# Memory values made whole in the first expert stage, and cross attention that turns X itself

## The reference, cut to what matters

```
def cross_attention(hn, mem_n, w_cq, w_ckv, w_co):
    q = (hn @ w_cq).reshape(B, S, 4, 256)
    k, v = split((mem_n @ w_ckv).reshape(B, 256, 2, 4, 256))
    s = einsum(q, k) * 256 ** -0.5          # per head, 512 x 256
    p = softmax(s)
    return einsum(p, v).reshape(B, S, 1024) @ w_co

h = h + (g_a * (y_a @ w_proj_a) + g_b * (y_b @ w_proj_b)) @ w_out
h = h + cross_attention(rmsnorm(h, norm_cross), rmsnorm(mem, norm_mem), w_cq, w_ckv, w_co)
```

## Time and profile before

| | |
|---|---|
| median of 3 runs | 2379.2 us (2378.73 to 2381.66) |
| span of the profiled execution | 2375.1 us |
| instructions | 27530 |
| PE busy | 2154.3 us (91%) |
| DVE busy | 699.1 us (29%) |
| ACT busy | 361.6 us (15%) |
| POOL busy | 128.6 us (5%) |
| DMA | 533.20 MB, mean 224 GB/s |
| mean granted TensorE clock | 0.970 |

### The profile page before, as it was taken

One profiled execution on the slowest core, in us unless ns is written; L12 is line 12 of the kernel. 1 busy time (PEld: TensorE's weight loads), 2 busy tenths in 40 slices (PEclk: granted clock), 3 DMA queues, 4 the chain that ended last, 5 costly groups with the idle time before them and its releaser, 6 DMA issues.

```text
span 2375.1 us, 27530 instructions
## 1 busy us (share of the span) xinstructions
PE 2154.3 (91%) x11887; PEld 1077.8 (45%) x11887; DVE 699.1 (29%) x1761; ACT 361.6 (15%) x692; POOL 128.6 (5%) x158
## 2 busy tenths in 40 slices
...
GB/s 295 71 36 71 68 4 159 160 204 373 422 427 427 427 426 428 381 269 67 2 29 3 73 2 36 87 121 120 106 142 80 211 418 426 426 428 426 427 428 274
DMA packets 94159, 533.20 MB, mean 224 GB/s; under 512 B 11169, under 2 KB 26198, under 8 KB 66635
## 3 DMA queue, kind: packets, MB, share of 16 engines
...
## 4 chain that ended last, share of the span: by engine, by line
PE 64%; DMA 28%; DVE 5%; issue 1%; ACT 1%; ACTq 0%; SPq 0%; DVEq 0%; POOLq 0%
PE ps L198 61%; DMA RING<-in_w 7%; DMA SC<-in_w 6%; DMA RING<-in_w_e_gate 4%; DMA RING<-in_w_e_up 4%; DMA SC<-in_w_e_down 3%; DMA XT<-in_w_e_down 1%; DMA XT<-in_w 1%; DMA RING<-in_w_ckv 1%; DMA RING<-in_w_proj_a 1%; PE ps L367 0%; PE ps L2924 0%; PE ps L2337 0%; DMA SC<-xrows,ST 0%; DMA RING<-ytab 0%
## 5 line engine op out<-in xcount | busy, mean ns | idle before, releaser
L198 PE MATMUL ps<-SC 64*64 64x64 f32 (+5 forms) x5912 | 698.0, 325 | 70.9 <-DMA RING<-in_w_e_up 15.3
L198 PE MATMUL ps<-RING,SC 128*64 128x512 f32 (+2 forms) x1856 | 656.4, 610 | 75.3 <-DMA RING<-in_w_e_gate 23.3
L198 PE MATMUL ps<-XT,RING 128*128 128x512 f32 (+1 forms) x1104 | 488.7, 595 | 2.8 <-DVE XT L194 1.1
L198 PEld LDWEIGHTS ps<-SC 64*64 64x64 f32 (+3 forms) x5912 | 339.2, 143 | 320.0 <-issue 297.3
L198 PEld LDWEIGHTS ps<-RING,SC 128*64 128x64 f32 (+2 forms) x1856 | 232.6, 155 | 367.6 <-issue 363.2
L198 PEld LDWEIGHTS ps<-XT,RING 128*128 128x128 f32 (+1 forms) x1104 | 204.6, 189 | 246.2 <-issue 241.4
L1709 DVE TENSOR_TENSOR SC<-SC,ps 128x512 f32<-128x512 f32 x32 | 22.0, 687 | 689.2 <-PE ps L198 689.2
L198 PE MATMUL ps<-XT,SC 128*64 128x512 f32 (+1 forms) x344 | 158.0, 612 | 9.3 <-DMA SC<-in_w_e_up 4.9
L198 PE MATMUL ps<-RING,XT 128*128 128x512 f32 (+1 forms) x384 | 147.5, 541 | 0.0
L198 PEld LDWEIGHTS ps<-RING,XT 128*128 128x128 f32 x384 | 67.5, 190 | 74.3 <-issue 73.8
L198 PE MATMUL ps<-SC,RING 128*128 128x512 f32 (+1 forms) x320 | 90.3, 451 | 6.1 <-DMA RING<-in_w_proj_a 6.1
...
## 6 DMA issues: line engine op xcount, KB each, us to landing
RING<-in_w SPq DMA_DIRECT2D x41, 2048.0 KB, 33.2
SC<-in_w SPq DMA_DIRECT2D x41, 2048.0 KB, 33.2
RING<-in_w_e_gate SPq DMA_DIRECT2D x22, 2048.0 KB, 33.9
SC<-in_w_e_down SPq DMA_DIRECT2D x17, 2048.0 KB, 33.2
RING<-in_w_in SPq DMA_DIRECT2D x16, 2048.0 KB, 8.6
SC<-in_w_e_up SPq DMA_DIRECT2D x15, 2048.0 KB, 33.2
XT<-in_w SPq DMA_DIRECT2D x10, 2048.0 KB, 34.3
SC<-in_w_e_gate SPq DMA_DIRECT2D x10, 2048.0 KB, 33.6
```

The source lines that it names most:

```text
L198: return e.matmul(out, l, r, start=st, stop=sp, skip_group_check=True)
```

## The change

**1. V's left half moves to stage 0.** `mv_s` is called a second time, before pair 8's loads, for "cv0", and `mv_p`, `mv_a` make four more blocks after pair 7. `memV` is twice as wide; `memT` is gone with its four writes, its read, the load of "cv0" between the output products' and the cross attention's weights, and the products in `cr_p`.

**2. X itself is turned.** PE transposes X, not the normed X, tile by tile beside the output products (`g2*15 cr g2*2 cr g2*2 cr*5` in the plan). Per tile DVE copies the left half in one instruction with the gains, ACT the right half in four of 128x128, and ACT then squares the tile. The row's factor is made beside the q products and goes into the softmax: times 1/16 as the exponent's scale, and negative into the maximum.

**3. Places.** The ring's turns before the cross attention drop their last four, and stage 1's turn is (0, 1, 8, 4, 7, 5, 2, 3, 6).

```
-        W.wait_ge(*ME.on("ev", "xt", 6))
-        W.wait_ge(*ME.on("ev", "xt", 7))
-        for n in range(4):
-            e.dma_start(memT[:, n, :], me_homes[n]).then_inc(*ME.up("dmt", "memT"))
...
-                if put_n == 6 * 4 and bi == 0:
-                    mv_s(e)
+                if put_n in (6 * 4, 6 * 8) and bi == 0:
+                    mv_s(e, put_n // 24 - 1)
...
-                if bi == 0 and q == 3:
-                    for n in range(4):
+                if bi == 0 and q in (3, 7):
+                    for n in range(q - 3, q + 1):
                         mv_p(e, c, n)
...
-        slots.begin((0, 1, 0, 1, 0, 1, 2, 3, 0, 1, 2, 3, 0, 1, 2, 3))
+        slots.begin((0, 1, 0, 1, 0, 1, 2, 3, 0, 1, 2, 3))
...
-        wload(e, "cv0", t["w_ckv_2"][0], 1024, 512, (CR, ("w", "cv0")))
...
 def cr_p(e):
-        W.wait_ge(*CR.on("mem"))
-        for half in range(1):
-            W.wait_ge(*slots.on(f"cv{half}"))
-            for j in range(2):
-                b, free = c.take("v", half, j)
...
-        turn_p(e, cr)
-        xt_ready(e, c)
+        for tt in range(NT):
+            for hf in range(2):
+                b, free = c.take("xt", tt, hf)
                 W.wait_ge(*free)
+                W.wait_ge(*G2.on("X", tt))
+                for j in range(4):
+                    i = e.transpose(b[:, j * 128:(j + 1) * 128], X[:, tt, (4 * hf + j) * 128:(4 * hf + j + 1) * 128], ident[:, :])
+                i.then_inc(*c.up("p", "xt", tt, hf))
+            if tt < NT - 1:
+                yield
...
 def cr_a(e):
-        e.dma_start(SC[:, 1, :], memT.rearrange("p a n -> p (a n)")).then_inc(*c.up("dmem"))
-        for n in range(4):
+        for n in range(8):
             W.wait_ge(*ME.on("memV", n))
-        e.dma_start(cr_V[:, :, 512:1024], memV).then_inc(*c.up("dmem"))
+        e.dma_start(cr_V, memV).then_inc(*c.up("dmem"))
...
+        W.wait_ge(*G2.on("mix", 7))
+        for tt in range(NT):
+            W.wait_ge(*c.on("xt", tt, 1))
+            for j in range(4):
+                copy_a(e, XT[:, 4 + j, tt * 128:(tt + 1) * 128], c.at("xt", tt, 1)[:, j * 128:(j + 1) * 128], cr_gain[:, 4 + j:5 + j]).then_inc(*c.up("a", "ev", "xt", tt, 1))
+            W.wait_ge(*G2.on("X", tt))
+            W.wait_ge(*c.last("a"))
+            e.activation(SC[:, 10, 0:D], X[:, tt, :], AF.Square, accum_out=cr_ss[:, tt:tt + 1]).then_inc(*c.up("a", "sq", tt))
+            if tt < NT - 1:
+                yield
...
-                e.activation(cr_pb[u % 8], c.at("s", u)[:, 0:256], AF.Exp, bias=s[:, 0:1], scale=0.0625, accum_out=s[:, 1:2]).then_inc(*c.up("a", "ev", "s", u))
+                e.activation(cr_pb[u % 8], c.at("s", u)[:, 0:256], AF.Exp, bias=s[:, 0:1], scale=cr_rs[:, qt:qt + 1], accum_out=s[:, 1:2]).then_inc(*c.up("a", "ev", "s", u))
...
 def cr_v(e):
-        norm_v(e, cr)
...
+        mean_rsq_v(e, c, cr_R, "nrm", cr_ss, 1.0 / D, 1e-6)
+        W.wait_ge(*c.on("nrm", "rs"))
+        e.tensor_scalar(cr_rs, cr_R.y, 0.0625, None, A.mult).then_inc(*c.up("v"))
+        e.tensor_scalar(cr_nrs, cr_R.y, -0.0625, None, A.mult).then_inc(*c.up("v"))
...
-                e.tensor_scalar(m, m, -0.0625, None, A.mult).then_inc(*c.up("v", "m", u))
+                e.tensor_scalar(m, m, cr_nrs[:, qt:qt + 1], None, A.mult).then_inc(*c.up("v", "m", u))
```

More of the change, by code:

```diff
@@ L236, in build @@
     ytab = nc.dram_tensor("ytab", [2 * T, D], F, kind="Internal").ap()
-    memT = nc.dram_tensor("memT", [128, 4, 512], F, kind="Internal").ap()
-    memV = nc.dram_tensor("memV", [128, 2, 512], F, kind="Internal").ap()
+    memV = nc.dram_tensor("memV", [128, 2, 1024], F, kind="Internal").ap()
     keysT = nc.dram_tensor("keysT", [128, 2, 1024], F, kind="Internal").ap()
@@ L1331, in mk_a, with mv_s @@
             keys_out(e, 0, me_K)
-    def mv_s(e):
-        s, free = slots.put(slots.next(), "cv1", (M0, ("mv", 3)))
+    def mv_s(e, half):
+        label = f"cv{half}"
+        s, free = slots.put(slots.next(), label, (M0, ("mv", 4 * half + 3)))
         for f in free:
             W.wait_ge(*f)
-        e.dma_start(s.rearrange("p (k n) -> p k n", k=8), t["w_ckv_2"][0].rearrange("(k p) n -> p k n", p=128)[:, :, 1536:2048]).then_inc(*slots.up("cv1"))
+        e.dma_start(s.rearrange("p (k n) -> p k n", k=8), t["w_ckv_2"][0].rearrange("(k p) n -> p k n", p=128)[:, :, 1024 + 512 * half:1536 + 512 * half]).then_inc(*slots.up(label))
     def mv_p(e, c, n):
-        W.wait_ge(*slots.on("cv1"))
+        label = f"cv{n // 4}"
+        W.wait_ge(*slots.on(label))
         b, free = c.take("mv", n)
         W.wait_ge(*free)
-        j, c0 = n // 2, n % 2 * 256
-        proj(e, b[:, 0:256], lambda k: me.dst[:, k, j * 128:(j + 1) * 128], lambda k: w8("cv1")[:, k, c0:c0 + 256], 8).then_inc(*c.up("p", "mv", n))
+        j, c0 = n % 4 // 2, n % 2 * 256
+        proj(e, b[:, 0:256], lambda k: me.dst[:, k, j * 128:(j + 1) * 128], lambda k: w8(label)[:, k, c0:c0 + 256], 8).then_inc(*c.up("p", "mv", n))
     def mv_a(e, c, n):
-        j, c0 = n // 2, n % 2 * 256
+        j, c0 = n % 4 // 2, n % 2 * 256
         dst = CH[:, c0:c0 + 256]
@@ L1355, in mv_a @@
         W.wait_ge(*c.on("ev", "mv", n))
-        e.dma_start(memV[:, j, c0:c0 + 256], dst).then_inc(*ME.up(f"dv{n % 2}", "memV", n))
+        c1 = n // 4 * 512 + c0
+        e.dma_start(memV[:, j, c1:c1 + 256], dst).then_inc(*ME.up(f"dv{n % 2}", "memV", n))
     def moe(bi, before, out, clear, first, ahead=None, pause=None):
@@ L2290, in re_g @@
         for n in range(4):
-            W.wait_ge(*ME.on("memV", n))
+            W.wait_ge(*ME.on("memV", 4 + n))
         e.memset(CH[:, :], 1.0).then_inc(*c.up("g"))
@@ L3157, in cr_a @@
         W.wait_ge(*TL.on("ya", 3))
-        W.wait_ge(*ME.on("memT"))
         for half in range(2):
             W.wait_ge(*ME.on("keysT", half))
-        e.dma_start(SC[:, 1, :], memT.rearrange("p a n -> p (a n)")).then_inc(*c.up("dmem"))
-        for n in range(4):
+        for n in range(8):
             W.wait_ge(*ME.on("memV", n))
-        e.dma_start(cr_V[:, :, 512:1024], memV).then_inc(*c.up("dmem"))
+        e.dma_start(cr_V, memV).then_inc(*c.up("dmem"))
         e.dma_start(SC[:, 2, :], keysT.rearrange("p a n -> p (a n)")).then_inc(*c.up("dmem", "mem"))
         yield
-        norm_a(e, cr)
-        for half in range(1):
-            W.wait_ge(*c.on("v", half, 0))
-            copy_a(e, cr_V[:, 0, half * 512:(half + 1) * 512], c.at("v", half, 0)[:, :]).then_inc(*c.up("a", "ev", "v", half, 0))
-        turn_a(e, cr)
+        W.wait_ge(*G2.on("mix", 7))
+        for tt in range(NT):
+            W.wait_ge(*c.on("xt", tt, 1))
[6 more added lines that the diff above has]
+                yield
         for half in range(2):
@@ L3177, in cr_a @@
             if u < NC_:
-                s = cr_st[u]
+                s, qt = cr_st[u], cr_units[u][1]
                 W.wait_ge(*c.on("m", u))
```

22 lines of the change are left out of this document (11 added, 11 removed), and 2 rows, old and new, of the table PLANS.

## The result

The changed kernel takes 2385.0 us (median of 8 runs, 2381.3 to 2386.6), the kernel before 2379.2 (8 runs beside it). The ratio is 1.0023, 95% interval 1.0014 to 1.0031: 5.5 us slower, between 3.3 and 7.4. The forecast was 2383.0. The profiled execution has a span of 2383.3 us, 8.2 more than the one before.

What follows compares the result with a forecast made beforehand. The prediction took bytes to bound both expert stages (426 and 427 GB/s) and PE the rest. Its terms, 6.7 + 7.5 - 1.2 - 9.2 = +3.8 us on a span of 2375.1, plus 4.1 to the median, gave 2383.0 us, range 2378.5 to 2387.

Steps and rivals of the forecast that it cites:

- Stage 0's bytes: Stage 0: cv0's load 4.9 us, its short runs 0.6, four memV writes 1.2; together +6.7 us, bounds 4.9 to 8.
- rival 4: Stage 0 runs dry at pair 9, its place being free 13.7 us late: 5 us, 2388; chance 0.05.
- The sign set for it: Stage 0: transfers falling below 420 GB/s behind pair 7 would show the forecast wrong.
- The held table: End of stage 0: pair 15's last w2 load holds the table's place, so the table goes out 7.05 us later; +7.5 us.
- The 0.4 us for the clock: End of stage 0: slower rows after PE's wait bring its sums to 1035.3 against ck1 at 1034.9; 0.4 us added.
- w_proj_a, -1.2: PE's wait for w_proj_a: it lands with the last of ACT's loads, now 0.52 MB less; -1.2 us, bounds 0 to -1.7.
- Up to q: Cross attention: V's left half gone, turns between output products, ACT's copies set the end; q begins 10.9 us earlier.
- The clock at q: Start of q: PE idles 3.3 us, then runs at 1.2 and not 2.4 GHz for a while; +1.7 us.
- The factor in the softmax: Attention units: exponent with a register column as scale, at most 0.09 us each, 16 times, beside other engines' work; nothing.
- Rival 1: Before q: PE's clock holds over the 3.3 us and ACT's copies are shorter; -1.7 to -2.5 us, 2381; chance 0.18.
- rival 2: End of stage 0: ck1 lands later still, as wl and rkv go out beside it; up to 3 us, 2386; chance 0.15.
- rival 3: End of stage 0: the table isn't held, so 7.5 us fall out; 2375.5; chance 0.07.

Runs made afterwards that it cites:

- k1: The changed kernel with stage 0's table rows in places 8 and 3 instead of 6 and 8, and ck1 in place 0 instead of 3: 2377.8 us, ratio 0.9995 to before.

## Why the prediction was right

The forecast was +3.8 us and the measurement is +5.5 (3.3 to 7.4). By its own terms:

- **Stage 0's bytes, +6.7.** Measured 467.2 - 460.5 = 6.7. Of its parts the load's bytes fit (4.3 for 1.84 MB), the writes are 0.9 for 0.49 MB against 1.2 for 0.52, the short runs at most 0.35 a load against 0.6. Those add up to 6.2, so that the sum comes out exactly is partly luck. The new products are hidden but for at most 0.9 us, and rival 4 is out: the stage has 426 GB/s from 700 to 1000. The sign set for it, under 420 GB/s behind pair 7, did show for 20 us (414), about as the kernel before has 414 and 412 around its own such load; it is no sign of a stage run dry. In the code the added load of stage 0 is the second one, as the labels cv0 and cv1 have changed places; bytes and shape are the same.
- **The held table, +7.5.** Measured 7.1: in all nine runs with both loads of V's weights in stage 0 and the table in places 6 and 8 it went out 7.11 to 7.13 us after the products began, in the five others at most 0.07, and changing the places alone took it away. The delay itself, 7.06 us, was forecast as 7.05. The 0.4 us for the clock did not come: the third tile's first four rows did take 3.78 us and not 1.88, but PE's sums still ended 0.4 us ahead of ck1's landing (1044.09 and 1044.48), where the forecast had them 0.4 us behind it.
- **w_proj_a, -1.2.** This term failed; measured +0.2. The step that failed: "so it came with the last of them, and 0.52 MB less are -1.2 us". In the kernel before it did not come with the last: keysT, issued 1.2 us behind it, landed 12.9 us after its own issue, so 1.2 us later than w_proj_a. Both queues moved the same number of pieces, so the rows' lengths set the shares: w_proj_a got a third beside rows of 8 KB and two thirds beside memV's rows of 2 KB. It was done when some 4.2 MB had moved, with the last 0.43 MB of keysT still to come. Now ACT's rows are all of 8 KB, w_proj_a is the last to land, and what is moved by then is again 4.2 MB. So most of the 0.52 MB that went had stood behind it. The row that could have told is in the trace of before: ACT's loads beside it landed at 6.8 (memT), 10.5 (memV) and 12.9 us, the last of them behind it:

```profile
SC<-keysT ACTq DMA_DIRECT2D x1, 1024.0 KB, 12.9
```

- **Up to q, -10.9.** Measured -11.85. ACT's four copies took 1.14 us and not 1.33, since they are 0.25 us apart and not 0.32; the order (ACT releases q, copies, square, copies) was as told.
- **The clock at q, +1.7.** 3.1 in this trace, 1.9 as the mean of eight. The rows it was taken from were one such draw.
- **The factor in the softmax, 0.** Measured +0.8. The step that failed: "at most 0.09 us each ... beside PE's and DVE's work; nothing". 0.09 is what an exponent takes more, and DVE's factor takes 0.06 more, which the forecast did not count. The units go round from PE to DVE to ACT and back, and of the 2.4 us that the 16 pairs cost 0.8 came through. Which of the two did it is not shown.

Together 6.7 + 7.1 + 0.2 - 11.85 + 1.9 + 0.8 = +4.85 us, inside the interval. The errors of the terms, -0.4, +1.4, -0.95, +0.2 and +0.8, leave 1 us. The path through the two stretches was right; that the two missed terms, +2.2 us together, were largely met by two others of -1.35 is luck. Rival 1 (the clock holds) happened in one trace of eight, rival 2 is refuted by k1, rival 3 by the table's issue in every run that has the change's places.
